# Sparse attention without per-item scaling, negated masks, and two inverses ahead of the delta rule

## The reference, cut to what matters

```python
score = jnp.where(causal, score, -inf); _, idx = lax.top_k(score, 128)   # 128 keys per query
s = einsum("qhd,qkd->qhk", qb, k[idx]) * HEAD_DIM ** -0.5                # 16 heads, one key head
s = where(valid, s, -inf)
p = softmax(s, axis=-1);  out = einsum("qhk,qkd->qhd", p, v[idx])
```

```python
decay = exp(where(tril, gc[..., :, None] - gc[..., None, :], -inf))
m = where(strict, einsum('cd,sd->cs', kb, kc) * decay, 0.0)
tmat = triangular_solve(m + eye, eye)          # the inverse, one for each chunk and head
qk = einsum('cd,sd->cs', qc, kc) * decay       # and then u, w and a scan over the chunks
```

## Time and profile before

| | |
|---|---|
| profiled execution: its time | 3422.1 us |
| its span | 3420.3 us |
| median of three runs | 3426.73 us |
| PE busy | 3258.1 us (95%), 18636 matmuls |
| DVE busy | 1721.0 us (50%) |
| ACT busy | 1263.2 us (37%) |
| POOL busy | 1183.5 us (35%) |
| DMA | 355.85 MB, mean 104 GB/s |
| mean granted PE clock | 0.987 of full |

### The profile page before, as it was taken

The page is one execution under the profiler, slowest core; times in us unless marked ns, Lnnn a source line. Parts: engine busy times, 40 slices in busy tenths (PEclk is TensorE's granted clock), DMA queues, the critical chain, the costliest instruction groups (busy, mean ns, idle before and its releaser), DMA issues.

```text
span 3420.3 us, 45148 instructions
## 1 busy us (share of the span) xinstructions
PE 3258.1 (95%) x18636; PEld 2568.0 (75%) x18636; DVE 1721.0 (50%) x3140; ACT 1263.2 (37%) x2247; POOL 1183.5 (35%) x950
## 2 busy tenths in 40 slices
PE   8999999987999999989899999999999998999998
PEld 3446888754678887865689888888887787878886
DVE  6754445679476666554567644122224329641123
ACT  3413232346443233655522233211113427743222
POOL 0143444553144442221266323222222341144443
PEclk9999999999999999999999999999999999999999
DMA  7523555310145553200344221212121211012222
GB/s 300 205 74 136 209 209 209 138 66 1 50 181 203 206 209 119 74 26 1 96 123 124 73 87 50 74 50 74 50 74 52 79 47 47 1 74 99 99 99 74
DMA packets 117292, 355.85 MB, mean 104 GB/s; under 512 B 42656, under 2 KB 85088, under 8 KB 92256
## 3 DMA queue, kind: packets, MB, share of 16 engines
q1 hardware_dynamic: 116224, 350.74, 28.4%
q10 hardware_dynamic: 864, 2.24, 0.2%
HBM read 339.75 MB, written 15.30 MB: 104 GB/s over the span
## 4 chain that ended last, share of the span: by engine, by line
PE 47%; DVE 5%; ACT 2%; POOL 1%; issue 1%; DMA 0%; SPq 0%; POOLq 0%; DVEq 0%; ACTq 0%
PE PSB L682 9%; PE PSB L686 9%; PE PSB L683 9%; PE PSB L1288 2%; PE PSB L1310 2%; PE PSB L1297 2%; PE PSB L2616 1%; PE PSB L2626 1%; PE PSB L2639 1%; PE PSB L2686 1%; PE PSB L731 1%; PE PSB L733 1%; PE PSB L732 1%; PE PSB L2593 1%; PE PSB L2195 1%
## 5 line engine op out<-in xcount | busy, mean ns | idle before, releaser
L686 PE MATMUL PSB<-R,WSR 128*128 128x512 f32 (+1 forms) x3084 | 1014.7, 366 | 0.0
L622 POOL TENSOR_TENSOR WSR<-SB,ahead 128x1024 fp32r<-128x1024 f32 x182 | 436.3, 2398 | 754.8 <-ACT ahead L599 718.8
L682 PE MATMUL PSB<-R,ahead 128*128 128x512 f32 (+1 forms) x1664 | 612.7, 368 | 4.2 <-POOL WSR L622 4.1
L683 PE MATMUL PSB<-R,ahead 128*128 128x512 f32 (+1 forms) x1664 | 592.8, 366 | 0.0
L686 PEld LDWEIGHTS PSB<-R,WSR 128*128 128x128 f32 x3084 | 533.1, 189 | 65.8
L682 PEld LDWEIGHTS PSB<-R,ahead 128*128 128x128 f32 x1664 | 313.0, 188 | 76.1 <-POOL WSR L622 5.7
L683 PEld LDWEIGHTS PSB<-R,ahead 128*128 128x128 f32 x1664 | 313.0, 188 | 52.9 <-issue 0.7
L622 POOL TENSOR_TENSOR WSR<-SB,ffn_weights 128x1024 fp32r<-128x1024 f32 x96 | 230.1, 2397 | 333.3 <-ACT ffn_weights L599 333.2
L682 PE MATMUL PSB<-R,ffn_weights 128*128 128x512 f32 x868 | 323.5, 373 | 1.0 <-POOL WSR L622 0.9
L683 PE MATMUL PSB<-R,ffn_weights 128*128 128x512 f32 x868 | 316.2, 372 | 0.0
L599 ACT ACTIVATE ahead<-SB 128x1024 fp32r<-128x1024 f32 x164 | 172.8, 1055 | 352.9 <-PE PSB L686 265.9
(11 more groups left out here) (443 smaller groups left out, 5772.7 us busy)
## 6 DMA issues: line engine op xcount, KB each, us to landing
SB<-in_w SPq DMA_DIRECT2D x95, 2048.0 KB, 8.0
SB<-in_ada SPq DMA_DIRECT2D x96, 1024.0 KB, 5.0
SB<-gate_rows SPq DMA_DIRECT2D x12, 512.0 KB, 4.1
whole_m<-SB SPq DMA_DIRECT2D x24, 256.0 KB, 3.4
SB<-whole_turned SPq DMA_DIRECT2D x12, 512.0 KB, 4.1
SB<-whole_inverse SPq DMA_DIRECT2D x12, 512.0 KB, 5.7
SB<-in_rpb SPq DMA_DIRECT2D x8, 448.0 KB, 3.9
spill<-SB SPq DMA_DIRECT2D x1, 3072.0 KB, 9.6
```

What stands on the lines that cost most here:

```text
L622: e.tt(lr, t, hf, ALU.subtract).then_inc(*G.up(("lo", self.e0 + j)))
L682: e.mm(b[:, 0:n], wh, xh[:, lo:lo + n], x == 0, False)
L683: e.mm(b[:, 0:n], wh, xl[:, lo:lo + n], False, False)
L686: ins = e.mm(b[:, 0:n], wl, xh[:, lo:lo + n], False, last)
```

## The change

Three things are changed.

1. Sparse attention (`late=range(8)`): the exponentials are no longer multiplied by the inverse of their sum. They go to the transposes and value products as they are (`ready_to_transpose` is `"exp"`). The sums of a pair's 8 items lie in one 128x8 tile; DVE takes one reciprocal for a pair. POOL spreads it to 128x512 (`WIDE`), PE turns it with 8 products against the identity into a transpose bank, and at the `done` step DVE copies it out (`OUT_`) and multiplies the pair's result with it. ACT's copy and DVE's rest take this product in place of the PSUM bank.
2. Masks and queries are negated, so that the minimum of the negated scores is the negative of the maximum: the extra instruction L1385 goes (sparse attention and the 32 neighbourhood items). The exponential has `scale=-1.0`. The query rest becomes a `scalar_tensor_tensor`.
3. Delta rule: both n=0 and n=1 are inverted inside the latent attention, `kk(2)`, `kq(0)` and their DVE parts are moved there too, the zeros are written a stage earlier, `decay_arg(3)` stands after the first `y` of n=0, and the weight panel waits for n=10 in place of n=9.

```diff
-                    e.act(self.slots(h)[0][1][y, :], self.queries(h)[y, :], ACT.Copy)
+                    e.act(self.slots(h)[0][1][y, :], self.queries(h)[y, :], ACT.Copy, scale=-1.0)
-                        v.tt(hi[1][other, :], self.queries(h)[y, :], hi[0][y, :], ALU.subtract)
+                        v.stt(hi[1][other, :], self.queries(h)[y, :], -1.0, hi[0][y, :], ALU.mult, ALU.subtract)
...
 # Attention.pe
-                        e.wait_ge(*st.at("p_scaled", t))
+                        e.wait_ge(*st.at(self.ready_to_transpose(t), t))     # "exp" where p in late
...
+                        if p in self.late and b == self.nqb - 1:             # behind the value products
+                            e.wait_ge(*st.at("wide", p))
+                            if u >= 2:
+                                e.wait_ge(*st.at("tbank", u - 2))
+                            for x in range(self.nqb):
+                                for hh in range(2):
+                                    e.mm(self.tbanks[u % 2][par(hh), col(x)],
+                                         self.WIDE[:, (4 * hh + x) * 64:(4 * hh + x) * 64 + 64], ident).then_inc(*P.up(("inverse_sums", p)))
+                            u += 1
 # Attention.act, at done
+                        if p in self.late:
+                            u += 1
+                            e.wait_ge(*st.at("out_scaled", p))
+                            source = self.OUT_
 # Attention.dve, at done, ahead of the maximum of item i
+                    if done is not None and self.chunks[done][0] in self.late:
+                        p = self.chunks[done][0]
+                        v.wait_ge(*st.at("inverse_sums", p))
+                        w = self.inverse_sums_at(p)
+                        if p - 1 in self.late:
+                            v.wait_ge(*st.at("attended", done - 1))
+                        v.cp(self.OUT_, self.tbanks[w % 2]).then_inc(*D.up(("tbank", w)))
+                        v.wait_ge(*D.now())
+                        v.tt(self.OUT_, self.obanks[done % len(self.obanks)], self.OUT_, ALU.mult).then_inc(*D.up(("out_scaled", p)))
...
-                            v.ttr(pb[:, 0:n], ps[:, 0:n], mask, 1.0, first, ALU.add, ALU.max, mx).then_inc(*D.up(("score_read", s)))
-                            v.wait_ge(*D.now())
-                            v.ts(mx, mx, -1.0, None, ALU.mult).then_inc(*D.up(("neg_max", s)))
+                            v.ttr(pb[:, 0:n], ps[:, 0:n], mask, 1.0, first, ALU.add, ALU.min, mx).then_inc(
+                                *D.up(("score_read", s), ("neg_max", s)))
...
+                    if x is not None and self.items[x][0] in self.late:      # in place of the reciprocal and scaling of item x
+                        p, hh, b = self.items[x]
+                        if (hh, b) == (1, self.nqb - 1):
+                            if p - 2 in self.late:
+                                v.wait_ge(*st.at("wide", p - 2))
+                            v.wait_ge(*st.at("exp", x))
+                            v.rec(self.INV[p % 2], self.SUMS[p % 2]).then_inc(*D.up(("inverse", p)))
 # Attention.pool
+                    if x is not None and self.items[x][0] in self.late and self.items[x][1:] == (1, self.nqb - 1):
+                        ...
+                        e.cp(self.WIDE.rearrange("p (x c) -> p x c", c=64),
+                             self.INV[p % 2].unsqueeze(2).broadcast_to([128, 8, 64])).then_inc(*G.up(("wide", p)))
...
 # even stage, SP                     # mla/gdn front, SP
+                gdn_front["zeros"](e)
-                zeros_sp(e)
                 gates_in(e, 0), gates_in(e, 1), blocks_sp(e, 0)
+                blocks_sp(e, 1)
                 gates_in(e, 2)
                 inverse_sp(e, 0)
-                blocks_sp(e, 1)
+                blocks_sp(e, 2)
                 gates_in(e, 3)
+                inverse_sp(e, 1)
...
-                e.wait_ge(*st.at("md", 9, 1, 6))
+                e.wait_ge(*st.at("md", 10, 1, 6))
 # front_pe: kk(0), kk(1) at steps 33, 46  ->  kk(0), kk(1), kk(2) at 33, 35, 45; kq(0) at 50
-                elif i in (36, 37): e.wait_ge(*st.at("mt", 0, i - 36))
+                elif i in (36, 37): e.wait_ge(*st.at("mt", 1, i - 36))
 # front_act: decay (0), (1), (2) at 33/34, 41/42, 45/46  ->  31/32, 33/34, 41/42
 # front_dve: decay_arg at 32, 40, 44, products at 35, 48  ->  30, 31, 40 and 34, 36, 47; scores(0) at 52
 # front_pool at 36: inverse(0)  ->  inverse(0), inverse(1)
 # gdn, PE: kk(2), kq(0), tokens(0)  ->  tokens(0)
 # gdn, DVE: products(2), scores(0), keys(0), values(0)  ->  keys(0), values(0)
-                    decay_arg(n + 3)
+                    if n:
+                        decay_arg(n + 3)
...
+                        if lv == 4 and n == 0:
+                            decay_arg(3)
```

More of the change, by code:

```diff
@@ L1267, in scratch, with inverse_sums_at, ready_to_transpose @@
                 sc = self.ST_[i % 6]
-                return [sc[:, j:j + 1] for j in range(4)]
+                mx, m2, s1, rc = [sc[:, j:j + 1] for j in range(4)]
+                p, hh, b = self.items[i]
+                if p in self.late:
+                    s1 = self.SUMS[p % 2][:, 4 * hh + b:4 * hh + b + 1]
+                return mx, m2, s1, rc
+            def inverse_sums_at(self, p):
+                before = self.items[:2 * self.nqb * (p + 1) + 1]
+                return self.u0 + sum(-(-self.nkeys(b) // 512) for _, _, b in before) + sum(x < p for x in self.late)
+            def ready_to_transpose(self, t):
+                return "exp" if self.items[t][0] in self.late else "p_scaled"
             def pe(self, e, hook=None):
@@ L1323, in act @@
                         ahead = [] if self.rest else [("attended", done)]
-                        e.act(self.out(p)[:, b0 * 128:b0 * 128 + n], self.obanks[done % len(self.obanks)][:, 0:n], ACT.Copy).then_inc(
+                        source = self.obanks[done % len(self.obanks)]
+                        if p in self.late:
+                            u += 1
+                            e.wait_ge(*st.at("out_scaled", p))
+                            source = self.OUT_
+                        e.act(self.out(p)[:, b0 * 128:b0 * 128 + n], source[:, 0:n], ACT.Copy).then_inc(
                             *A.up(("out_hi", done), *ahead))
@@ L1342, in act @@
                         n = self.mask(h, b)
+                        if p - 2 in self.late and p in self.late:
+                            e.wait_ge(*st.at("inverse", p - 2))
                         e.wait_ge(*st.at("neg_max", s))
@@ L1402, in pool @@
             def pool(self, e, hook=None):
-                st = self.st
-                for i, _, _, _, _, _ in self.steps():
+                st, G = self.st, self.st.pool
+                for i, _, x, _, _, _ in self.steps():
                     if hook:
                         hook(i)
+                    if x is not None and self.items[x][0] in self.late and self.items[x][1:] == (1, self.nqb - 1):
+                        p = self.items[x][0]
+                        if p - 1 in self.late:
+                            e.wait_ge(*st.at("inverse_sums", p - 1))
+                        e.wait_ge(*st.at("inverse", p))
+                        e.cp(self.WIDE.rearrange("p (x c) -> p x c", c=64),
+                             self.INV[p % 2].unsqueeze(2).broadcast_to([128, 8, 64])).then_inc(*G.up(("wide", p)))
         class HeadNorm:
@@ L1552, in dsa @@
                             lambda h, b: (128 * (b + 1), MK[b], [st.at("mask", b)]),
-                            lambda p: H[p][1], lambda h: [st.at("q_lo", h)], parts=parts, rest=lambda p: H[p][2])
+                            lambda p: H[p][1], lambda h: [st.at("q_lo", h)], parts=parts, rest=lambda p: H[p][2], late=range(8), wide=HQ[0:2])
             acc, SQ = QT[0], QT[1:3]
@@ L2556, in kq @@
                     if n < 12:
[L2557 to L2562 removed]
+                        kq_pe(e, n)
                 def tokens(n, i):
@@ L2779, in products_dve, with scores_dve @@
                     *D.up(("mt", n, y), ("read", n, "kk", y)))
+            def scores_dve(v, n, y):
+                d = n % 2
+                v.wait_ge(*st.at("kq", n, y))
+                if n >= 2:
+                    v.wait_ge(*st.at("o_sum", n - 2))
+                av = AT[d].rearrange("p (x two c) -> p x two c", two=2, c=128)[:, :, y, :]
+                v.tt(av, g3(bank(n, "kq", y)), g3(dec(n)[:, y * 512:(y + 1) * 512]), ALU.mult).then_inc(
+                    *D.up(("at", n, y), ("read", n, "kq", y)))
             def front_dve(v, i):
-                if i in (32, 40, 44):
-                    decay_arg_dve(v, (32, 40, 44).index(i))
-                elif i in (35, 48):
+                if i in (30, 31, 40):
+                    decay_arg_dve(v, (30, 31, 40).index(i))
+                elif i in (34, 36, 47):
                     for y in range(2):
-                        products_dve(v, 0 if i == 35 else 1, y)
```

(15 more changed lines are left out.)

97 lines of the change are left out of this document (48 added, 49 removed).

## The result

The changed kernel takes 3408.66 us (median of four runs, 3403.89 to 3409.52), the kernel before 3425.27 us (median of four). The ratio is 0.995, 95% interval 0.9932 to 0.9967: faster by 11 to 23 us. The forecast was 3412 us, with 3399 to 3423 as the range. The mechanisms were right. Some sizes were off, and the experiments show that one part of the change costs time which another part had already gained.

The account below looks back on a forecast made before the run. DVE was taken to bound the sparse attention and neighbourhood items, PE the latent attention except at waits for gates. Gains of 1.7 + 2.9 + 9.2 = 13.8 us from 3426.7 gave 3412.9, leaning to 3412; range 3399 to 3423.

Parts of the forecast that it names:

- The pair: Sparse attention, steady part: a 3.68 us chain at `done` makes a pair 11.5 us against 11.28, 1.3 us lost for six.
- DVE's saving doesn't reach the end: Sparse attention, steady pairs: the new chain through three engines at `done` takes all that DVE saves.
- The start: Sparse attention up to the first result: fewer reciprocals and scalings on DVE, less the first chain, net 1.0 us gained.
- the tail: Sparse attention, seventh result to the projection's first product: 11.6 us before, 2.0 us gained, ends 0 and 2.6.
- Stage: Whole sparse attention: -1.3 + 1.0 + 2.0 = 1.7 us gained, ends 5 lost and 7 gained.
- The masks: 32 neighbourhood items of the last layer: DVE's queue 0.09 us shorter an item, 2.9 us gained, ends 0 and 6.1.
- The front: Delta rule's front, gates plus chunk loop start: 4.4 + 4.8 = 9.2 us gained, ends 2 and 15.
- (a): Latent attention: gates go out 5.4 us earlier, `kk(0)`'s 3.49 us wait and the half clock behind it go, 4.4 us gained.
- (b): Chunk loop's start: product behind d comes 17.0 us after the release instead of 22.1, 4.8 us gained, ends 0 and 8.
- A: Sparse attention: the chain at `done` doesn't hold ACT, a pair takes 10.1 us, total 3402 us; chance 0.14.
- B: Delta rule's front: waits for gates move rather than go, 3.5 us gained instead of 9.2, total 3418.5 us; chance 0.20.
- C: Sparse attention: the hold at `done` idles PE and the clock falls, slower, full price 3440 us; chance 0.06.

Follow-up runs that it names:

- experiment 3: The changed kernel with the exponentials scaled item by item again, signs and front as changed: 3401.75 us, ratio 0.9932.
- experiment 4: The kernel before with the unscaled exponentials and turned sums alone, no sign turned, front as before: 3423.01 us, ratio 0.9991.
- experiment 5: The changed kernel with PE turning the inverse sums ahead of the transposes and value products of the same step: 3399.97 us, ratio 0.9929.
- experiment 8: The changed kernel with the zeros written back ahead of the first gates in SP's queue: 3416.92 us, ratio 0.9982.
- `front_only`: The kernel before with the third part alone (delta rule's front and the zeros): 3413.81 us, ratio 0.9969.
- experiment 1: Same run as `front_only`: the kernel before with the third part alone, 3413.81 us, ratio 0.9969.
- experiment 9: The changed kernel with the argument of n=3 moved behind the first d of n=0 on DVE: 3405.1 us.
- experiment 6: Changed kernel, sums turned ahead of the value products, ACT's result copy behind its step's transposed copy and exponential: 3415.21 us, ratio 0.9973.
- `copy_behind`: Same run as experiment 6: ACT's result copy behind the exponential, on the kernel of experiment 5, 3415.21 us, ratio 0.9973.

## Why the prediction was right, and where it was off

**The pair.** The chain was put at 3.68 us and measured 3.60; the pair at 11.5 (11.1 to 11.95) and measured 11.63; ACT's wait at 1.9 us, measured 2.47, because ACT finds its other inputs ready and reaches it earlier (its work outside the chain takes 8.03 us, between the 7.46 and 8.27 of the bounds). "DVE's saving doesn't reach the end" is what experiments 3 to 5 show. Six pairs lost 2.1 us where 1.3 was forecast. The start gained 2.1 (from the last search of the top-k to the first result it is 28.7 us before and 26.6 after) for a forecast of 1.0, and the tail 2.4 for 2.0. Stage: 2.4 gained, forecast 1.7. How near this comes is partly luck: in `front_only`, whose code is the same here as before, the start took 2.2 us and six pairs 3.4 us more than in the profile before.

What the prediction did not do is to price the parts against each other. It set the new chain against the old pair of 11.28 us, though the signs, in the same change, take 0.77 us off that pair. Against what the signs alone reach the turned sums are a loss of 6 to 7 us, hidden in the sum.

**The masks.** This is the term that was mis-sized: 0.09 us an item, measured 0.18, and 2.9 us in all, measured 5.1 (from the first to the last of the 32 masked items 81.0 us before and 75.9 after). This pair of profiles flatters it: with the sign change the three profiles have 79.8 to 81.0 us, without it the eleven have 75.9 to 77.7, and the means differ by 3.8 us. The step said that the queue gets "about 0.09 us shorter". It took the sign change's start (2856.54) to the reciprocal's (2856.61) and left out the gap ahead of the sign change. That gap is 0.12 us from the start of the read of the accumulator. The sign change waits there by a semaphore for its own engine's result; the reciprocal needs nothing of it and starts together with the read once the sign change is gone. The Trainium skill (VectorE: DVE Perf Modes, "The DRAIN you can't avoid") says that in a chain of eight copies on DVE a semaphore behind each cost nothing extra. Behind this read the dependent instruction came 0.12 us later than an independent one, so here the measurement decides.

**The front.** Forecast 9.2 us; in the profiles it is 9.8 (the stages ahead were 1.1 us late, the chunk loop ended 8.7 to 8.8 early), alone 11.4 by the medians. (a) From SP's release to the last scores 4.7 us were gained against 4.4 forecast; experiment 8 confirms that the place of the zeros is part of the cause. (b) From there to the first product for u, near the end of chunk step n=0, it is 30.2 us after and 34.8 before, 4.6 gained against 4.8. Inside it two errors cancel: the gates landed 11.9 us after the release and not 13.5, and the product behind d came after 15.4 and not 17.0, but the clock was at half for nearly all of the 7 us behind. The forecast had said that this might fall on more work. So the size of (b) is right by luck: in `front_only`, with the same code, the clock stayed at 1.00 behind a wait of 2.87 us, and it took 27.7 us, a gain of 7.1. Its last product for u came 1.7 us earlier after the release than in the changed kernel (256.0 us, 257.7 there), and with it the 9.8 become 11.5, where the medians show 11.4 for the front alone.

**The sum.** The touched stages gained 2.4 + 5.1 + 9.8 = 17.3 us, forecast 13.8. The span shrank by 13.9 only, since the profiled execution of the changed kernel came 2.8 us later to the last search of the top-k, in code that nobody touched, and lost 0.7 more between the sparse and the latent attention. Over the fourteen profiles of this study that same point lies between 782.4 and 787.4 us. The medians, 16.6 us apart, are nearer the 17.3.

**The rivals.** A is refuted by ACT's wait in all pairs. B is refuted by experiment 1. C did not happen in the changed kernel (1.00 over the six pairs, and the same in the profiles of experiments 8 and 9, which leave this stage as it is), but experiment 6 shows it to be real. The code before stands on that edge too: in the execution of `front_only`, whose sparse attention is that of the kernel before, two of seven pairs ran at 0.86. Two neighbouring stretches of it, each one pair:

```profile
827.62:839.00 11.38, 9.17 (x77) 6.51 (x77) 10.51 (x44) 9.34 (x28) 0.00 (x0) 1.00 0.01 2
839.00:851.17 12.17, 10.15 (x74) 7.33 (x74) 10.62 (x43) 9.22 (x29) 0.00 (x0) 0.86 0.01 2
```

Two more pairs of that execution took 11.96 us at a granted clock of 1.00; why stays open. So part of what the signs gained may be a PE that idles less and keeps its clock; no run separates that. The Trainium skill (TensorE: Matmul & The Clock Gate, "HAM oscillation — how this bites in real kernels") tells of a loop that waits for a DMA longer than it works, and whose clock falls anew in each round. These rows agree in kind only: no single wait is longer than 0.8 us here and 1.3 us in experiment 6, PE is busy for about 81% of a pair, and the clock falls in some pairs and not in others.

## What to carry to other kernels

Taking work off the bounding engine pays only down to the next one, and a chain through three engines at one step costs each in-order queue in it what that queue can't fill with other work (of 3.60 us ACT waited 2.47): measure it from release to release, and shorten it by starting what doesn't depend on the last input (here 0.83 us off the chain were 0.84 us off each pair). Price the parts of a change against each other, not each against the kernel before. When a gain of a few us has to be told from noise, compare the stretch of the profile that the edit touches, not only medians taken at different times. To see what a small dependent instruction costs, count from the start of what it depends on to the start of the next independent one (0.19 us in the earlier trace rows, where 0.18 was gained), not its own start-to-start time.

## What the runs showed that I had not expected

- A one-element instruction that needs the result just read from DVE's accumulator cost its queue 0.18 us an item, 0.12 of it ahead of its start.
- Moving a waiting copy later in its queue made the kernel 15 us slower, as another engine waited for it ahead of its own critical work (1.68 us, ahead of the maximum).
- With waits of PE of at most 0.8 us (`front_only`) and 1.3 us (`copy_behind`) at a time, some pairs ran at a clock of 0.86 to 0.87 and took 0.8 to 1.3 us more than a steady pair of their kernel at the full clock, with the same work. Others behind the same kind of gap did not.
- ACT's copy of 128x512 took 630 ns from SBUF in the changed kernel (616 where it stood behind the exponential) and 576 ns from PSUM.
